# RMSNorm statistics of a decoder trunk: token rows in pieces of 128, 128 and 8 instead of three times 88

## Chip, cores and metric

The kernel runs on one core of one Trainium2 chip. The metric is the device time of one execution in microseconds, the median over several runs. A profiled execution gives, beside its time, a trace of every instruction of that core.

## What is computed

One inference step of a four-layer decoder trunk over 256 prompt tokens and 8 decode tokens, 264 in all, with a model width of 1024 and float32 weights. Each layer has three sublayers: a half feed-forward block, a token mixer (short convolution, sparse attention, differential attention, convolution again, by layer), and a second half feed-forward block. There are 12 sublayers. Each has an RMSNorm ahead of it and one behind it, which makes 24 norms:

```python
def rms_norm(x, g):
    xf = x.astype(jnp.float32)
    y = xf * lax.rsqrt(jnp.mean(xf * xf, axis=-1, keepdims=True) + EPS)
    return (y * g.astype(jnp.float32)).astype(x.dtype)

def half_ffn(x, g_pre, g_post, w_in, w_out):
    gate, up = jnp.split(rms_norm(x, g_pre) @ w_in, 2, axis=-1)
    return x + 0.5 * rms_norm((jax.nn.silu(gate) * up) @ w_out, g_post)
...
        xp = xp + rms_norm(yp, g[3])
        xs = xs + rms_norm(ys, g[3])
```

The norm's scale is one number per token, `rsqrt(mean of squares + EPS)`.

## The kernel before

**Layout.** Activations stand with the model width on the 128 partitions, in 8 chunks, and the 264 tokens along the free dimension. A sublayer is a row of matrix products with tokens as the moving operand. Weights stream in from memory in units of 512 columns by four chunks. ScalarE rounds each unit to a high part (`w_high_ring`), VectorE subtracts to get the low part (`w_low_ring`, line 864), and TensorE forms each product from three matmuls, high by high, high by low, low by high (lines 1391 to 1393). All engines follow programs written out by hand in five blocks, one per engine, that meet at semaphores. The order within an engine is the order of its program.

**A norm in five steps.** Each norm has a number: even ones are the norm ahead of a sublayer (the pre norm), odd ones the norm behind it (the post norm).

- *Statistics*, TensorE, `norm_stats`, line 1399. The squares summed over chunks (`sum_pre` or `sum_post`, plus for a post norm the last chunk of `sq`) are the stationary operand, and a column of 1/1024 (`mean_col`) is the moving one. The result is a column of token means in PSUM, tokens on partitions. The 264 tokens are cut into three columns of `NT` = 88 rows. A post norm does this twice, once for `sum_post` and once for `sq`. Each float32 matmul leaves two records in the profile, so three matmuls are six records.
- *Variance*, VectorE, `norm_var`, line 908. One instruction adds EPS to the 88 by 3 block and signals `var_ready`.
- *Power*, GpSimd (POOL in the profile), line 618. One instruction raises the 88 by 3 block to the power -1/2 into `rs` and signals `rs_ready`. GpSimd's program does the norms in order, and ahead of a pre norm's power it adds up the squares of `x` chunk by chunk (line 584).
- *Broadcast*, TensorE, `norm_bcast`, line 1408. For each third of the tokens, a matmul with the `rs` column repeated 128 times as the stationary operand and the identity as the moving one puts every token's scale on all 128 partitions, tokens along the free dimension again. Only the last of the three signals `bcast_done`.
- *Use*, VectorE. For a pre norm, `norm_copy` (lines 914 and 915) copies the scales from PSUM to `r_pre`, and the drains of the first products multiply with it. For a post norm, line 1365 scales `y` straight from PSUM, and line 1371 adds it to `x`.

**What stands around them.** A pre norm works beside products: the statistics follow the products of the sublayer's first group, and the broadcast stands in TensorE's program behind the first 48 matmuls of the second group. VectorE forms two more low parts (line 864) between the variance and the copy. A post norm is a dead end: nothing of the next sublayer can start before `x` is updated. TensorE runs matmuls that nobody reads (`keep_running`, line 1415), 9 ahead of the broadcast and 13 behind it.

Of the kernel before, what the change touches and what calls it, by code (L numbers as in the profile page):

```python
# [26 lines left out]
ALU = mybir.AluOpType  # L27
# [3 lines left out]
P = 128  # L31
D_MODEL = 1024
SEQ = 256
DEC = 8
T = SEQ + DEC
# [8 lines left out]
EPS = 1e-6  # L44
# [78 lines left out]
def trunk_kernel(nc, x_prompt, x_sample, state_conv, cache_nsa, state_nsa_win, cache_diff, page_table,  # L123
# [12 lines left out]
    with ctx:  # L136
# [333 lines left out]
        def bcast_out(norm, k):  # L470

            b = norm_bank(norm)
            if norm % 2:
                return ps[:, b, 8 + NT * k:8 + NT * k + NT]
            return ps[:, b + k // 2, 320 + NT * (k % 2):320 + NT * (k % 2) + NT]

        tok_stores = {"nsa": 6, "diff": 9}

# [34 lines left out]
        @block.gpsimd  # L513
        def _(pool):
            fill = lambda t, v: nc.gpsimd.memset(t, v).then_inc(pool_step, 1)
            fill(ident[:, :], 0.0)
            pool.wait_ge(pool_step, 1)
            nc.gpsimd.affine_select(out=ident[:, :], in_=ident[:, :], compare_op=ALU.not_equal, fill=1.0, base=0,
                                    pattern=[[-1, P]], channel_multiplier=1).then_inc(ident_ready, 1)
            fill(cmp_ok[:, :, :], 1.0)  # L520
            fill(head_of_row[:, :], 1.0)
            fill(block_of_row[:, :], 1.0)
            fill(tmp[:, 0, 0:256], 0.0)
            fill(tmp[:, 1, 0:256], 0.0)
            fill(tmp[:, 2, 0:32], 0.0)
            fill(mean_col[:, 0:1], 1.0 / D_MODEL)
            fill(mean_col[:, 1:2], 1.0 / P)
            fill(minus_half[:, :], -0.5)
            fill(var[:, :], 1.0)
            fill(small[:, :], 1.0)  # L530
            fill(even_tmp[:, :], 0.0)
            n = [13]
            pool.wait_ge(pool_step, n[0])

            def select(t, pattern, op, fill, base, mult):

                nc.gpsimd.affine_select(out=t, in_=t, compare_op=op, fill=fill, base=base,
                                        pattern=pattern, channel_multiplier=mult).then_inc(pool_step, 1)
                n[0] += 1
                pool.wait_ge(pool_step, n[0])  # L540

            def copy(dst, src):
                nc.gpsimd.tensor_copy(dst, src).then_inc(consts_ready, 1)

            pool.wait_ge(ident_ready, 1)
            copy(ident_b[:, :], ident[:, :])

            select(tmp[:, 0, 0:P], [[-1, P]], ALU.is_ge, NEG, 0, 1)
            copy(causal[:, :], tmp[:, 0, 0:P])

            select(cmp_ok[:, :, :], [[P, 2], [-CMP_BLOCK, N_CMP]], ALU.is_ge, 0.0, -(CMP_BLOCK - 1), 1)
            nc.gpsimd.tensor_scalar(cmp_bias[:, :, :], cmp_ok[:, :, :], -1.0, -NEG, ALU.add, ALU.mult)\
                .then_inc(consts_ready, 1)

            select(head_of_row[:, :], [[-N_CMP, 16]], ALU.is_ge, 0.0, 0, 1)
            select(head_of_row[:, :], [[N_CMP, 16]], ALU.is_ge, 0.0, N_CMP - 1, -1)

            select(block_of_row[:, :], [[-CMP_BLOCK, 4]], ALU.is_ge, 0.0, 0, 1)
            select(block_of_row[:, :], [[CMP_BLOCK, 4]], ALU.is_ge, 0.0, CMP_BLOCK - 1, -1)
            fill(block_strip[:, :], 0.0)  # L560
            n[0] += 1
            pool.wait_ge(pool_step, n[0])
            copy(block_strip[:, 28:32], block_of_row[:, :])

            select(even_tmp[:, :], [[-2, 64]], ALU.not_equal, 1.0, 0, 1)

            view = tmp[:, 1, 0:256].rearrange("p (j n) -> p j n", n=N_CMP)
            select(view, [[-4, 32], [0, N_CMP]], ALU.is_ge, NEG, 0, 1)
            select(view, [[4, 32], [0, N_CMP]], ALU.is_ge, NEG, 3, -1)
            copy(own_cmp[:, :, :], view)  # L570

            view = tmp[:, 2, 0:32].rearrange("p (g b) -> p g b", b=DEC)
            select(view, [[-4, GROUPS], [-16, DEC]], ALU.is_ge, NEG, 0, 1)
            select(view, [[4, GROUPS], [16, DEC]], ALU.is_ge, NEG, 3, -1)
            copy(own_new[:, :, :], view)
            for norm in range(2 * len(subs)):
                s = subs[norm // 2]
                if norm % 2 == 0:

                    for c in range(1, NC):  # L580
                        pool.wait_ge(x_squared, NC * s.i + c + 1)
                        if c > 1:
                            pool.wait_ge(pre_summed, (NC - 1) * s.i + c - 1)
                        nc.gpsimd.tensor_tensor(sum_pre[:, :], sum_pre[:, :] if c > 1 else sq[:, 0, :], sq[:, c, :],
                                                ALU.add).then_inc(pre_summed, 1)
                if s.kind == "nsa" and norm % 2:

                    for b in range(s.cache_units):
                        t = stage_of["c", s.cache0 + b]
                        pool.wait_ge(loaded[t % RING], 32 * (t // RING + 1))  # L590
                        if b == 0:
                            pool.wait_ge(dec_q, s.attend + 1)
                        if b >= 2:
                            pool.wait_ge(cache_turned, pieces_to(s.cache0 + b - 2))
                        if b < DEC:
                            page = wstage[:, t % RING, :, :].rearrange("p (t g) (h c) -> p t (g h) c", t=2, c=256)
                            keys = page[:, :, :, 128:192]
                        else:
                            keys = wstage[:, t % RING, 0:2, :].rearrange("p t (g c) -> p t g c", g=GROUPS)[:, :, :, 0:HEAD]
                        nc.gpsimd.tensor_copy(k_pairs[:, b % 2, :, :, :], keys).then_inc(keys_paired, 1)  # L600
                if s.cache_units and norm % 2:

                    pool.wait_ge(at_scaled, task0[s.kind] + len(TASKS[s.kind]))
                    pool.wait_ge(tok_stored, 16 * tok_stores[s.kind])
                    nc.gpsimd.memset(pt_wide[0][:, :, :], 0.0).then_inc(wide_zeroed, 1)
                    if s.kind == "nsa":
                        pool.wait_ge(cache_scored, pieces_to(2 * DEC - 1))
                        nc.gpsimd.memset(pt_wide[1][:, :, :], 0.0).then_inc(wide_zeroed, 1)
                if s.kind == "diff" and norm % 2:

                    pool.wait_ge(sub_var, 1)
                    nc.gpsimd.tensor_tensor(sub_r, sub_v, minus_half[:, 0:16], ALU.pow).then_inc(sub_rs, 1)
                    pool.wait_ge(sub_var, 2)
                    nc.gpsimd.tensor_tensor(s_nmx[0][0:64, :], s_mx[0][0:64, :], minus_half[0:64, 0:1], ALU.pow)\
                        .then_inc(sub_rs, 1)

                pool.wait_ge(var_ready, norm + 1)
                nc.gpsimd.tensor_tensor(rs[0:NT, :], var[0:NT, :], minus_half[0:NT, 0:3], ALU.pow).then_inc(rs_ready, 1)  # L618


        @block.scalar
# [237 lines left out]
        def _(dve):  # L859
# [44 lines left out]
            def norm_var(norm):  # L904

                dve.wait_ge(stats_done, norm + 1)
                b, col = norm_bank(norm), stat_col(norm)
                V.tensor_scalar(var[0:NT, :], ps[0:NT, b, col:col + 3], EPS, None, ALU.add).then_inc(var_ready, 1)  # L908

            def norm_copy(s):  # L910

                dve.wait_ge(bcast_done, 2 * s.i + 1)
                b = norm_bank(2 * s.i)
                V.tensor_copy(r_pre[:, 0:2 * NT], ps[:, b, 320:320 + 2 * NT]).then_inc(rstd_ready, 1)
                V.tensor_copy(r_pre[:, 2 * NT:T], bcast_out(2 * s.i, 2)).then_inc(rstd_ready, 1)
                dve.wait_ge(rstd_ready, 2 * (s.i + 1))

            def low_x(s, c):
# [463 lines left out]
        def _(pe):  # L1382
# [12 lines left out]
            def norm_stats(norm, squares, first=True, last=True):  # L1395

                b, col = norm_bank(norm), stat_col(norm)
                for k in range(3):
                    mm = MM(ps[0:NT, b, col + k:col + k + 1], squares[:, NT * k:NT * k + NT], mean_col[:, 0:1],
                            start=(norm % 2 == 1 and first and k == 0), stop=last, skip_group_check=True)  # L1400
                if last:
                    mm.then_inc(stats_done, 1)

            def norm_bcast(norm):

                pe.wait_ge(rs_ready, norm + 1)
                for k in range(3):
                    mm = MM(bcast_out(norm, k), rs[0:NT, k:k + 1].broadcast_to([NT, P]), ident[0:NT, 0:NT],  # L1408
                            start=(norm % 2 == 1 and k == 0), stop=True, skip_group_check=True)
                mm.then_inc(bcast_done, 1)  # L1410

# [596 lines left out]
```

## Time and profile before

| what | value |
|---|---|
| median of 3 runs | 2265.44 us (2263.7 to 2267.54) |
| the profiled execution's own time | 2265.54 us |
| its span, first to last instruction | 2263.8 us |
| TensorE matmuls busy | 2175.4 us (96% of the span) |
| VectorE busy | 1447.8 us (64%) |
| ScalarE busy | 948.4 us (42%) |
| GpSimd busy | 173.4 us (8%) |
| mean granted TensorE clock | 0.991 of full speed |

The busy time of an engine counts each moment once, however many instructions overlap in it. Matmuls overlap their neighbours, so the duration of one is more than the time that it adds to the stream. For the norms, the timeline of one norm says more than the busy shares: a step costs what lies between its start and the start of the step that waits for it.

### The profile page before, as it was taken

The page shows a single profiled execution, that of the slowest core. Times are in us where ns is not written, and L with a number is a line of the kernel's source. Part 1 is how long each engine was busy: PE and PEld are TensorE (multiplying, and loading weights), DVE is VectorE, ACT ScalarE, POOL GpSimd, SP SyncE. Part 2 cuts the span into 40 slices and gives each one's busy share as a digit, 9 for nine tenths or more (in the row PEclk, how much of TensorE's full clock was granted, in tenths as well). Part 3 has the DMA queues.
Part 4 walks back from the last instruction along what each step waited for, and adds up shares of the span by engine and source line. Part 5 has one row for each costly group of instructions (what it writes and reads, how often), then busy time and mean ns, then how long its engine had stood idle before and what let it go on. Part 6 is the DMA issues. An engine that isn't in the chain of part 4 may idle for free.

```text
span 2263.8 us, 42724 instructions
## 1 busy us (share of the span) xinstructions
PE 2175.4 (96%) x17890; PEld 2091.6 (92%) x17890; DVE 1447.8 (64%) x1677; ACT 948.4 (42%) x1111; POOL 173.4 (8%) x165
## 2 busy tenths in 40 slices
PE   7999999999999989999999999779999999999997
PEld 7999999999999955799999999469999999999997
DVE  6764877647755568477567646657765765677753
ACT  4434354434444335344445434325444444435432
POOL 3000120002001000020020002002001100202000
PEclk9999999999999999999999999999999999999999
DMA  7554446554653543455455554324654654455550
GB/s 229 188 189 147 164 151 211 173 179 151 200 176 123 177 132 122 160 162 195 153 165 189 176 182 163 131 73 133 197 184 140 202 183 163 142 186 169 185 179 27
DMA packets 286125, 370.83 MB, mean 164 GB/s; under 512 B 12247, under 2 KB 212360, under 8 KB 285924
## 3 DMA queue, kind: packets, MB, share of 16 engines
q1 hardware_dynamic: 282378, 364.57, 48.9%
q10 hardware_dynamic: 3610, 4.28, 0.5%
q8 instruction: 105, 1.72, 0.3%
q14 instruction: 32, 0.26, 0.0%
HBM read 364.87 MB, written 8.11 MB: 165 GB/s over the span
## 4 chain that ended last, share of the span: by engine, by line
PE 45%; issue 9%; DVE 8%; ACT 1%; POOL 1%; POOLq 0%; DVEq 0%; ACTq 0%
PE ps L1391 13%; PE ps L1393 13%; PE ps L1392 13%; DVE y L1365 1%; DVE x L1371 1%; PE ps L1613 1%; DVE probs L1141 1%; DVE kt_dec L1194 1%; DVE w_low_ring L864 1%; PE ps L1603 1%; PE ps L1570 1%; ACT w_high_ring L634 1%; PE ps L1408 0%; POOL rs L618 0%; DVE small L1127 0%
## 5 line engine op out<-in xcount | busy, mean ns | idle before, releaser
L864 DVE TENSOR_TENSOR w_low_ring<-wstage,w_high_ring 128x2048 fp32r<-128x2048 f32 x332 | 732.1, 2230 | 280.8 <-ACT w_high_ring L634 200.9
L1391 PE MATMUL ps<-x_hi,w_high_ring 128*128 128x264 f32 x3112 | 888.4, 285 | 3.5 <-DVE w_low_ring L864 3.5
L1393 PE MATMUL ps<-x_hi,w_low_ring 128*128 128x264 f32 x3112 | 884.9, 284 | 0.0
L1392 PE MATMUL ps<-x_lo,w_high_ring 128*128 128x264 f32 x3112 | 883.7, 284 | 0.0
L1391 PEld LDWEIGHTS ps<-x_hi,w_high_ring 128*128 128x128 f32 x3112 | 586.5, 188 | 4.1 <-issue 4.1
L1392 PEld LDWEIGHTS ps<-x_lo,w_high_ring 128*128 128x128 f32 x3112 | 588.0, 189 | 0.0
L1393 PEld LDWEIGHTS ps<-x_hi,w_low_ring 128*128 128x128 f32 x3112 | 586.8, 189 | 0.0
L1391 PE MATMUL ps<-h_hi,w_high_ring 128*128 128x264 f32 x1664 | 473.5, 285 | 0.6 <-issue 0.6
L1393 PE MATMUL ps<-h_hi,w_low_ring 128*128 128x264 f32 x1664 | 473.8, 285 | 0.0
L1392 PE MATMUL ps<-h_lo,w_high_ring 128*128 128x264 f32 x1664 | 472.4, 284 | 0.0
L634 ACT ACTIVATE w_high_ring<-wstage 128x2048 fp32r<-128x2048 f32 (+2 forms) x172 | 307.9, 1817 | 306.9 <-PE ps L1393 288.8
L1391 PEld LDWEIGHTS ps<-h_hi,w_high_ring 128*128 128x128 f32 x1664 | 313.1, 188 | 1.2 <-issue 1.2
L1392 PEld LDWEIGHTS ps<-h_lo,w_high_ring 128*128 128x128 f32 x1664 | 313.9, 189 | 0.2 <-issue 0.2
L1393 PEld LDWEIGHTS ps<-h_hi,w_low_ring 128*128 128x128 f32 x1664 | 313.3, 188 | 0.0
L805 ACT ACTIVATE w_high_ring<-wstage 128x2048 fp32r<-128x2048 f32 x160 | 302.1, 1907 | 16.3 <-PE ps L1393 16.1
L641 ACT ACTIVATE tmp<-tmp 128x528 f32<-128x528 f32 x88 | 57.0, 648 | 398.9 <-DVE tmp L888 398.9
L618 POOL TENSOR_TENSOR rs<-var,minus_half 88x3 f32<-88x3 f32 x24 | 68.5, 2853 | 1704.9 <-DVE var L908 1704.9
L643 ACT ACTIVATE h_hi<-tmp 128x528 f32 (+1 forms) x88 | 56.8, 646 | 144.6 <-DVE tmp L898 144.6
L888 DVE TENSOR_TENSOR tmp<-ps,r_pre 128x528 f32<-128x528 f32 x88 | 62.1, 706 | 82.3 <-PE ps L1393 82.1
L901 DVE TENSOR_TENSOR h_lo<-tmp,h_hi 128x528 f32 (+1 forms) x88 | 62.4, 709 | 81.5 <-ACT h_hi L643 81.5
L1444 PE MATMUL ps<-x_hi,w_high_ring 128*128 128x264 f32 x384 | 99.0, 288 | 7.0 <-ACT x_hi L649 3.8
L1445 PE MATMUL ps<-x_hi,w_low_ring 128*128 128x264 f32 x384 | 97.8, 285 | 0.0
(285 smaller groups left out, 1827.3 us busy)
## 6 DMA issues: line engine op xcount, KB each, us to landing
wstage<-in_ffn_w_in_dram SPq DMA_DIRECT2D x352, 512.0 KB, 5.1
wstage<-in_ffn_w_out_dram SPq DMA_DIRECT2D x160, 512.0 KB, 4.6
wstage<-in_conv_w_in_dram SPq DMA_DIRECT2D x48, 512.0 KB, 4.8
wstage<-in_nsa_w_in_dram SPq DMA_DIRECT2D x20, 512.0 KB, 4.9
wstage<-in_ffn_w_out_dram SPq DMA_DIRECT2D x32, 256.0 KB, 2.8
wstage<-in_conv_w_out_dram SPq DMA_DIRECT2D x16, 512.0 KB, 5.0
wstage<-in_cache_nsa_dram SPq DMA_DIRECT2D x16, 512.0 KB, 4.5
wstage<-in_diff_w_in_dram SPq DMA_DIRECT2D x16, 512.0 KB, 5.2
```

Of the source, the lines that this page charges most:

```text
L618: nc.gpsimd.tensor_tensor(rs[0:NT, :], var[0:NT, :], minus_half[0:NT, 0:3], ALU.pow).then_inc(rs_ready, 1)
L634: nc.scalar.activation(w_high_ring[:, u % RING, 0:n, 0:cols], wstage[:, t % RING, 0:n, 0:cols], ACT.Copy).then_inc(w_high, 1)
L641: nc.scalar.activation(tanh_t, gate_t, ACT.Tanh, scale=0.5).then_inc(tanh_done, 1)
L805: nc.scalar.activation(w_high_ring[:, u % RING, :, :], wstage[:, t % RING, :, :], ACT.Copy).then_inc(w_high, 1)
L864: V.tensor_tensor(w_low_ring[:, u % RING, 0:n, 0:cols], wstage[:, stage_of["w", u] % RING, 0:n, 0:cols], w_high_ring[:, u % RING, 0:n, 0:c ...
L888: V.tensor_tensor(gate_t, ps[:, 4 * psum_set:4 * psum_set + 2, 0:T], b3(r_pre[:, :], 2), ALU.mult)\
L901: V.tensor_tensor(h_lo[:, chunk, :], prod_t, h_hi[:, chunk, :].bitcast(F32), ALU.subtract)\
L1391: MM(out, wh, hi, start=first, stop=False)
L1392: MM(out, wh, lo, start=False, stop=False)
L1393: return MM(out, wl, hi, start=False, stop=last)
L1444: MM(out(tile), w(w_high_ring, tile), x_hi[:, c, :], start=(c == 0), stop=False)
L1445: MM(out(tile), w(w_low_ring, tile), x_hi[:, c, :], start=False, stop=False)
```

## The change

The tokens are cut as the rest of the kernel cuts them, by `TOK`: prompt tokens 0 to 127, prompt tokens 128 to 255, and the 8 decode tokens. Columns 0 and 1 of `var` and `rs` then have 128 rows, and column 2 has 8 rows. The variance is two VectorE instructions, the 8 by 1 block first, then 128 by 2. The power is two GpSimd instructions, 128 by 2 first, then 8 by 1, each with its own signal. The power still waits for both variance instructions. The first two broadcast matmuls wait for the first power, the last one for the second.

```diff
         def bcast_out(norm, k):
 
             b = norm_bank(norm)
+            t0, n = TOK[k]
             if norm % 2:
-                return ps[:, b, 8 + NT * k:8 + NT * k + NT]
-            return ps[:, b + k // 2, 320 + NT * (k % 2):320 + NT * (k % 2) + NT]
+                return ps[:, b, 8 + t0:8 + t0 + n]
+            return ps[:, b + (k > 0), 320 + P * (k > 1):320 + P * (k > 1) + n]
...
-                pool.wait_ge(var_ready, norm + 1)
-                nc.gpsimd.tensor_tensor(rs[0:NT, :], var[0:NT, :], minus_half[0:NT, 0:3], ALU.pow).then_inc(rs_ready, 1)
+                pool.wait_ge(var_ready, 2 * (norm + 1))
+                nc.gpsimd.tensor_tensor(rs[:, 0:2], var[:, 0:2], minus_half[:, 0:2], ALU.pow).then_inc(rs_ready, 1)
+                nc.gpsimd.tensor_tensor(rs[0:DEC, 2:3], var[0:DEC, 2:3], minus_half[0:DEC, 0:1], ALU.pow)\
+                    .then_inc(rs_ready, 1)
...
-                V.tensor_scalar(var[0:NT, :], ps[0:NT, b, col:col + 3], EPS, None, ALU.add).then_inc(var_ready, 1)
+                V.tensor_scalar(var[0:DEC, 2:3], ps[0:DEC, b, col + 2:col + 3], EPS, None, ALU.add).then_inc(var_ready, 1)
+                V.tensor_scalar(var[:, 0:2], ps[:, b, col:col + 2], EPS, None, ALU.add).then_inc(var_ready, 1)
...
-                V.tensor_copy(r_pre[:, 0:2 * NT], ps[:, b, 320:320 + 2 * NT]).then_inc(rstd_ready, 1)
-                V.tensor_copy(r_pre[:, 2 * NT:T], bcast_out(2 * s.i, 2)).then_inc(rstd_ready, 1)
+                V.tensor_copy(r_pre[:, 0:P], bcast_out(2 * s.i, 0)).then_inc(rstd_ready, 1)
+                V.tensor_copy(r_pre[:, P:T], ps[:, b + 1, 320:320 + T - P]).then_inc(rstd_ready, 1)
...
-                for k in range(3):
-                    mm = MM(ps[0:NT, b, col + k:col + k + 1], squares[:, NT * k:NT * k + NT], mean_col[:, 0:1],
+                for k, (t0, n) in enumerate(TOK):
+                    mm = MM(ps[0:n, b, col + k:col + k + 1], squares[:, t0:t0 + n], mean_col[:, 0:1],
                             start=(norm % 2 == 1 and first and k == 0), stop=last, skip_group_check=True)
...
-                pe.wait_ge(rs_ready, norm + 1)
-                for k in range(3):
-                    mm = MM(bcast_out(norm, k), rs[0:NT, k:k + 1].broadcast_to([NT, P]), ident[0:NT, 0:NT],
+                for k, (t0, n) in enumerate(TOK):
+                    pe.wait_ge(rs_ready, 2 * norm + (2 if n == DEC else 1))
+                    mm = MM(bcast_out(norm, k), rs[0:n, k:k + 1].broadcast_to([n, P]), ident[0:n, 0:n],
                             start=(norm % 2 == 1 and k == 0), stop=True, skip_group_check=True)
```

TensorE at a post norm, before, from the statistics to the first product of the next sublayer (a matmul's first operand here is the moving one, the second the stationary one, and the size is the output's):

```order
L1399 MATMUL ps<-mean_col,sum_post 88x1 [waits y_copied,post_added]
L1399 MATMUL ps<-mean_col,sum_post 88x1 x2
L1399 MATMUL ps<-mean_col,sq 88x1 [waits y_squared]
L1399 MATMUL ps<-mean_col,sq 88x1 x2
L1415 MATMUL ps<-own_cmp,ident_b 128x256 [waits y_copied]
L1415 MATMUL ps<-own_cmp,ident_b 128x256 x8
L1408 MATMUL ps<-ident,rs 128x88 [waits rs_ready]
L1408 MATMUL ps<-ident,rs 128x88 x2
L1415 MATMUL ps<-own_cmp,ident_b 128x256 x13
L1444 MATMUL ps<-x_hi,w_high_ring 128x264 [waits x_high,w_low,psum_drained]
```

The same place after the change:

```order
L1403 MATMUL ps<-mean_col,sum_post 128x1 [waits y_copied,post_added]
L1403 MATMUL ps<-mean_col,sum_post 128x1
L1403 MATMUL ps<-mean_col,sum_post 8x1
L1403 MATMUL ps<-mean_col,sq 128x1 [waits y_squared]
L1403 MATMUL ps<-mean_col,sq 128x1
L1403 MATMUL ps<-mean_col,sq 8x1
L1419 MATMUL ps<-own_cmp,ident_b 128x256 [waits y_copied]
L1419 MATMUL ps<-own_cmp,ident_b 128x256 x8
L1412 MATMUL ps<-ident,rs 128x128 [waits rs_ready] x2
L1412 MATMUL ps<-ident,rs 128x8 [waits rs_ready]
L1419 MATMUL ps<-own_cmp,ident_b 128x256 x13
L1448 MATMUL ps<-x_hi,w_high_ring 128x264 [waits x_high,w_low,psum_drained]
```

The number of matmuls stays, their shapes change, and the last broadcast matmul has a wait of its own. GpSimd, before, from the first pre norm on:

```order
L584 TENSOR_TENSOR sum_pre<-sq 128x264 [waits x_squared]
L584 TENSOR_TENSOR sum_pre<-sum_pre,sq 128x264 [waits pre_summed,x_squared] x6
L618 TENSOR_TENSOR rs<-var,minus_half 88x3 [waits var_ready] x2
L584 TENSOR_TENSOR sum_pre<-sq 128x264 [waits x_squared]
L584 TENSOR_TENSOR sum_pre<-sum_pre,sq 128x264 [waits pre_summed,x_squared] x6
```

And after the change:

```order
L585 TENSOR_TENSOR sum_pre<-sq 128x264 [waits x_squared]
L585 TENSOR_TENSOR sum_pre<-sum_pre,sq 128x264 [waits pre_summed,x_squared] x6
L619 TENSOR_TENSOR rs<-var,minus_half 128x2 [waits var_ready]
L620 TENSOR_TENSOR rs<-var,minus_half 8x1
L619 TENSOR_TENSOR rs<-var,minus_half 128x2 [waits var_ready]
L620 TENSOR_TENSOR rs<-var,minus_half 8x1
L585 TENSOR_TENSOR sum_pre<-sq 128x264 [waits x_squared]
```

A pair of instructions stands where one stood, and the second of the pair waits for nothing. On VectorE the pair of variance instructions (lines 911 and 912) stands where line 908 stood, with one wait ahead of the first.

## Rows read from the trace of the kernel before

**Rows 1.** The page: span, busy times, TensorE clock in 40 slices.
```profile
span 2263.8 us, 42724 instructions
PE 2175.4 (96%) x17890; PEld 2091.6 (92%) x17890; DVE 1447.8 (64%) x1677; ACT 948.4 (42%) x1111; POOL 173.4 (8%) x165
...
PEclk9999999999999999999999999999999999999999
```

**Rows 2.** Line 618, all 24 powers, and who waited for them.
```profile
L618 POOL TENSOR_TENSOR rs<-var,minus_half x24: 846/1850/5042, 35.8 to 2243.8; 88x3 f32<-88x3 f32 x24
...
  PEld ps L1408: 5.4, 12
  PE ps L1408: 2.1, 12
```

**Rows 3.** Waits: who waited for whom, us in total, times, longest.
```profile
DVE y L1365 <- PE ps L1408: 24.0, 12, 2.0
...
PE ps L1391 <- DVE w_low_ring L864: 3.5, 11, 0.3
```

**Rows 4.** Timeline, first post norm, TensorE matmuls: start us, us, instruction.
```profile
216.56 0.63 PE L1399 MATMUL ps<-mean_col,sum_post 128*88 128x1 f32 x6 [0.22 <-DVE sum_post L1356]
217.05 0.61 PE L1399 MATMUL ps<-mean_col,sq 128*88 128x1 f32 x6
217.52 1.14 PE L1415 MATMUL ps<-own_cmp,ident_b 128*128 128x256 bf16 x9
218.84 0.90 PE L1408 MATMUL ps<-ident,rs 88*128 88x88 f32 x6 [0.18 <-POOL rs L618]
219.58 1.58 PE L1415 MATMUL ps<-own_cmp,ident_b 128*128 128x256 bf16 x13
221.51 0.36 PE L1444 MATMUL ps<-x_hi,w_high_ring 128*128 128x264 f32 x1 [0.35 <-ACT x_hi L649]
```

**Rows 5.** Timeline, first post norm, TensorE weight loads.
```profile
216.56 0.54 PEld L1399 LDWEIGHTS ps<-mean_col,sum_post 128*88 128x88 f32 x6 [0.43 <-DVE sum_post L1356]
217.02 0.55 PEld L1399 LDWEIGHTS ps<-mean_col,sq 128*88 128x88 f32 x6
217.44 0.94 PEld L1415 LDWEIGHTS ps<-own_cmp,ident_b 128*128 128x128 bf16 x9
218.84 0.74 PEld L1408 LDWEIGHTS ps<-ident,rs 88*128 88x128 f32 x6 [0.46 <-POOL rs L618]
219.47 1.41 PEld L1415 LDWEIGHTS ps<-own_cmp,ident_b 128*128 128x128 bf16 x13
```

**Rows 6.** Timeline, first post norm, VectorE and GpSimd.
```profile
217.69 0.16 DVE L908 TENSOR_SCALAR var<-ps 88x3 f32<-88x3 f32 x1 [1.19 <-PE ps L1399]
219.86 0.49 DVE L1365 SCALAR_TENSOR_TENSOR y<-y,gains,ps 128x264 f32<-128x264 f32 x1 [2.01 <-PE ps L1408]
...
217.93 0.86 POOL L618 TENSOR_TENSOR rs<-var,minus_half 88x3 f32<-88x3 f32 x1 [179.31 <-DVE var L908]
```

**Rows 7.** Timeline, GpSimd, the two other powers of the program.
```profile
1502.40 2.93 POOL L612 TENSOR_TENSOR small<-small,minus_half 128x16 f32<-128x16 f32 x1 [8.97 <-DVE small L1295]
1512.91 0.54 POOL L614 TENSOR_TENSOR small<-small,minus_half 64x1 f32<-64x1 f32 x1 [7.58 <-DVE small L1308]
```

**Rows 8.** Timeline, GpSimd, instructions close behind one another.
```profile
2.24 0.12 POOL L515 MEMSET minus_half<- 128x32 f32 x1
2.30 0.10 POOL L515 MEMSET var<- 128x3 f32 x1
2.33 0.34 POOL L515 MEMSET small<- 128x288 f32 x1
...
18.16 2.08 POOL L584 TENSOR_TENSOR sum_pre<-sq 128x264 f32<-128x264 f32 x1 [9.46 <-ACT sq L650]
20.39 7.16 POOL L584 TENSOR_TENSOR sum_pre<-sum_pre,sq 128x264 f32<-128x264 f32 x6
```

**Rows 9.** Timeline, second pre norm, TensorE.
```profile
233.36 0.56 PE L1399 MATMUL ps<-mean_col,sum_pre 128*88 128x1 f32 x6
240.11 0.80 PE L1408 MATMUL ps<-ident,rs 88*128 88x88 f32 x6
```

**Rows 10.** Timeline, second pre norm, VectorE and GpSimd.
```profile
234.84 5.04 POOL L618 TENSOR_TENSOR rs<-var,minus_half 88x3 f32<-88x3 f32 x1 [3.82 <-DVE var L908]
...
234.61 0.16 DVE L908 TENSOR_SCALAR var<-ps 88x3 f32<-88x3 f32 x1
234.69 4.48 DVE L864 TENSOR_TENSOR w_low_ring<-wstage,w_high_ring 128x2048 fp32r<-128x2048 f32 x2
```

**Rows 11.** Third pre norm: GpSimd, then TensorE.
```profile
335.48 5.04 POOL L618 TENSOR_TENSOR rs<-var,minus_half 88x3 f32<-88x3 f32 x1 [3.20 <-DVE var L908]
...
341.37 0.80 PE L1408 MATMUL ps<-ident,rs 88*128 88x88 f32 x6
```

## The prediction

> **What bounds the kernel.** I read the page first, for the engines' shares. TensorE is busy 96% of the span at a clock in the top tenth throughout [rows 1], so most of the run is a stream of matmuls that the change doesn't touch. What the norms cost is what they add between two stretches of that stream. The view of line 618 says where: of the 24 powers only 12 have TensorE waiting for them [rows 2], and the waits show VectorE waiting 24.0 us in 12 pieces for the broadcast ahead of line 1365 [rows 3], 2.0 us for each of the 12 post norms. The timeline of one post norm shows the chain [rows 4, 6]: statistics from 216.56, variance at 217.69, power from 217.93 to 218.79, broadcast from 218.84, scaling at 219.86. That is 3.30 us, nearly all of it serial, and nothing useful runs beside it; TensorE fills its part with matmuls of line 1415 and then waits for `x_hi` until 221.51. So whatever the chain gains or loses is gained or lost twelve times, in full. The pre norms are read from two further timelines [rows 9 to 11].
>
> **The sum at a post norm**, term by term.
>
> *Statistics.* A matmul has two records. Their pace is set by the weight loads: twelve records with 88 weight columns take 217.44 - 216.56 = 0.88 us, 0.073 each, while six with 128 weight columns (the broadcast) take 219.47 - 218.84 = 0.63, 0.105 each [rows 5]. After the change there are eight records with 128 columns and four with 8: 8 x 0.105 = 0.84, plus four short ones, for which no row stands. Their bounds are 0 and 0.073 each. I take about the middle, 0.04, which makes 1.00 us and **+0.12 us**, with bounds of -0.04 and +0.25.
>
> *Variance.* Two VectorE instructions instead of one. At the second pre norm the next instruction starts 0.08 us behind the variance (234.61, then 234.69) though the variance lasts 0.16 [rows 10]. So the second one costs **+0.08**, at most 0.16.
>
> *First power.* The program has three sizes of power that run undisturbed: one element per partition in 0.54 us and sixteen in 2.93 [rows 7], three in 0.86 [rows 6], 0.846 at the least [rows 2]. The first two give 2.39 / 15 = 0.159 us per element, and from there 0.54 + 2 x 0.159 = 0.86 for three, as measured, though these rows have 64, 128 and 88 partitions. So partitions are free, and each power carries 0.38 us whatever its size. Two elements are 0.70 us: **-0.16**.
>
> *Second power.* 0.54 us by the nearest row, one element [rows 7]. Unlinked instructions on GpSimd start 0.06 us before their predecessor's record ends (2.24 + 0.12 against 2.30), and linked adds stand apart by 20.39 - (18.16 + 2.08) = 0.15 [rows 8]. The second power is unlinked: 0.54 - 0.05 = **+0.49**. The lower end is a single element's slope of 0.16 with the fixed part hidden; the upper end is a whole power of today's price behind a gap, 0.85 + 0.15 = 1.00.
>
> *Broadcast.* Today the scaling starts 219.86 - 218.79 = 1.07 us behind the power [rows 6]. After the change only the two records of the 8-token matmul stand behind the second power. Four records fewer are 4 x 0.105 = -0.42 [rows 5]. A moving operand of 8 columns also ends sooner: the statistics, with one moving column, release VectorE 0.17 us after TensorE has gone on to line 1415 (217.52 to 217.69), the broadcast with 88 columns 0.28 us (219.58 to 219.86) [rows 4, 6]. That is another -0.11, so **-0.53** in all, with bounds of -0.42 (nothing for the shorter operand) and -0.64 (one record's 0.105 more, should the two short records also follow closer).
>
> This term has a floor beneath it. The two prompt matmuls start 0.05 us behind the first power (218.79 to 218.84) and have four records, 4 x 0.105 + 0.02 = 0.44. The last matmul can't start earlier than 0.49 us behind the first power, so a second power shorter than 0.44 brings nothing more.
>
> The sum is 0.12 + 0.08 - 0.16 + 0.49 - 0.53 = **0.00 us** for each post norm. The low ends together, with the floor, are -0.04 + 0.08 - 0.16 + 0.44 - 0.64 = -0.32; the high ends 0.25 + 0.16 - 0.16 + 1.00 - 0.42 = +0.83. In words: the broadcast that is hidden was about as long as the fixed cost of the instruction that hides it.
>
> A rule of the Trainium skill speaks for more than this. The page "GPSIMD Engine Reference", section 2.1 (Instruction dispatch), says that completion doesn't hold back the next Pool instruction: each of the eight cores goes on as soon as its own share is done. By it the second power would begin inside the first one's record and cost well under its 0.49. No row here has two powers back to back, so the trace can't say. By the rule alone the sum would fall to the floor, 0.05 us lower per post norm and 0.6 us in all.
>
> **The pre norms.** The power lasts 5.04 us there instead of 0.85, and ends 0.71 us after VectorE's two low parts do (239.88 against 239.17) [rows 10]; VectorE, which then waits for the broadcast, takes up nothing between. So the power is held until these end, and the second power follows in a free stretch. The Trainium skill's page "SBUF — State Buffer", on engine ports, calls this an exclusive lock on a port pair that the two engines share; by that rule, the trace agrees. With the change, VectorE's low parts end 0.08 later, the first power is 0.16 shorter, and the second adds 0.49: `rs` is complete 0.41 us later, at 240.29. TensorE comes to the broadcast at 240.11 and to its last matmul four records later, 240.53 [rows 9]. The cover is 0.24 us. Two of the 12 pre norms are that tight; elsewhere, as at the third, the power ends 0.85 us ahead of TensorE [rows 11]. The longer statistics (six records, +0.06) fall into the 0.3 us that TensorE then waits for a low part, 11 times [rows 3]. The broadcast keeps six records at 128 weight columns. The two copies of 128 and 136 columns replace 176 and 88, the same sum. I cost the pre norms at **0**; if the cover went, 0.1 to 0.3 us each at a few of them.
>
> **Total.** 12 x 0.00 + 0 = 0. The sum is made against the profiled execution's 2265.54 us (span 2263.8), which is 0.1 us from the median of 2265.44. The forecast is **2265.5 us**.
>
> **The rivals.**
>
> *A. The second power costs a whole start.* GpSimd takes it up only when the first is done with, and its real price is near the upper end, 1.00 us. Everything else at my values, that is +0.51 per post norm, 12 x 0.51 = 6.1 us: 2271.6 us, slower. It decides from about 0.87 us for the second power, where 12 x 0.38 reaches 4.5 us. For it: the fixed part of 0.38 us is real. Against it: 0.54 us for one element already holds that part, and gaps on GpSimd are at most 0.15. Chance 9%.
>
> *B. The broadcast doesn't start behind the first power.* If the signal of the first power came only with the second, all six records would stand behind both, as today: the -0.53 falls away, +0.53 per post norm, 6.4 us: 2271.9 us. Nothing in the rows shows it; each instruction here releases its own waiter. Chance 4%.
>
> *C. The low ends meet.* Short statistics records, the floor reached, a short last broadcast: -0.32 per post norm, 3.8 us, 2261.7 us. For it: 8 weight columns may load in next to nothing. Against it: three terms would have to lie at their ends. To be beyond what can be measured it needs another 0.06 each. The chance that it goes that far, something that I don't see included, is 9%.
>
> **How the numbers follow.** A measurement of this kernel can tell about 0.2%, 4.5 us, from no change; that is 0.38 us per post norm, and my sum has to be wrong by that much, in one direction, at all twelve. The forecast of no measurable change has 78%, A and B together 13% (slower), C 9% (faster). The range takes in C nearly whole (-3.5 us) and reaches up to +4.8 us, since the unknown second power and the statistics can err further upward than down: 2262.0 to 2270.3 us. A's and B's own values lie outside and hold the rest.
>
> **What would show it.** In the changed profile a post norm should read: twelve statistics records in about 1.0 us; two variances 0.08 apart; a first power of 0.70; a second of 0.54 starting within 0.1 of the first one's end; four broadcast records beside it; line 1369 starting about 0.5 us behind the second power; and from the first statistics record to that line 3.3 us as before. The wait of VectorE for the broadcast should keep about 2.0 us. At pre norms TensorE should wait for no power. I'm wrong if the second power lasts clearly more than 0.54 or starts late, if the four prompt records begin only behind it, or if 12 pre norms show an idle TensorE ahead of line 1412.

## The result and the profile after

| what | before | after |
|---|---|---|
| median of 11 runs each | 2267.14 us | 2271.55 us |
| lowest and highest | 2263.33 to 2269.38 | 2269.47 to 2273.55 |
| profiled execution: time, span | 2265.54, 2263.8 us | 2273.55, 2271.8 us |
| mean granted TensorE clock | 0.991 | 0.990 |

The changed kernel is slower, by about a quarter of a percent: the ratio is 1.0027, with a 95% interval of 1.0018 to 1.0035. That is 6.1 us of 2267, between 4.1 and 7.9. (The recorded ratio isn't the quotient of the two medians. These lie 4.4 us apart, inside the same interval.) The profiled execution after is the slowest of its eleven, so its 8.0 us over the one before are partly scatter. Steps are compared below, not spans.

The first post norm after the change, TensorE's matmuls, then its weight loads (start us, us, instruction), which answer to [rows 4, 5]:

```profile
218.28 0.73 PE L1403 MATMUL ps<-mean_col,sum_post 128*128 128x1 f32 x6 [0.22 <-DVE sum_post L1360]
218.94 0.73 PE L1403 MATMUL ps<-mean_col,sq 128*128 128x1 f32 x6
219.60 1.16 PE L1419 MATMUL ps<-own_cmp,ident_b 128*128 128x256 bf16 x9
220.76 1.02 PE L1412 MATMUL ps<-ident,rs 128*128 128x128 f32 x6
221.71 1.59 PE L1419 MATMUL ps<-own_cmp,ident_b 128*128 128x256 bf16 x13
```

```profile
218.27 0.63 PEld L1403 LDWEIGHTS ps<-mean_col,sum_post 128*128 128x128 f32 x6 [0.43 <-DVE sum_post L1360]
218.93 0.63 PEld L1403 LDWEIGHTS ps<-mean_col,sq 128*128 128x128 f32 x6
219.59 0.88 PEld L1419 LDWEIGHTS ps<-own_cmp,ident_b 128*128 128x128 bf16 x9
220.75 0.93 PEld L1412 LDWEIGHTS ps<-ident,rs 128*128 128x128 f32 x6 [0.28 <-POOL rs L619]
221.71 0.33 PEld L1419 LDWEIGHTS ps<-own_cmp,ident_b 128*128 128x128 bf16 x4
```

The same place on VectorE and GpSimd, which answers to [rows 6]:

```profile
219.70 0.14 DVE L911 TENSOR_SCALAR var<-ps 8x1 f32<-8x1 f32 x1 [1.49 <-PE ps L1403]
219.78 0.14 DVE L912 TENSOR_SCALAR var<-ps 128x2 f32<-128x2 f32 x1
221.90 0.49 DVE L1369 SCALAR_TENSOR_TENSOR y<-y,gains,ps 128x264 f32<-128x264 f32 x1 [1.98 <-PE ps L1412]
...
219.99 0.71 POOL L619 TENSOR_TENSOR rs<-var,minus_half 128x2 f32<-128x2 f32 x1 [177.99 <-DVE var L912]
220.66 0.54 POOL L620 TENSOR_TENSOR rs<-var,minus_half 8x1 f32<-8x1 f32 x1
```

Variances, powers and signals did what was forecast: 0.08 us between the variances, a first power of 0.71 us, a second of 0.54 that starts 0.04 before the first one's end, and a broadcast that begins 0.06 behind the first power. Both surprises are on TensorE. The statistics take 219.70 - 218.28 = 1.42 us up to the variance, before 217.69 - 216.56 = 1.13. And the second power ends at 221.20, but the scaling starts only 0.70 us later, at 221.90, where 0.54 had been forecast.

The waits show the statistics over all 12 post norms (us in total, times, longest), after the change and then before it:

```profile
DVE y L1369 <- PE ps L1412: 23.6, 12, 2.0
DVE var L911 <- PE ps L1403: 19.2, 12, 1.8
```

```profile
DVE var L908 <- PE ps L1399: 16.4, 12, 1.7
```

VectorE waits 19.2 us ahead of the variance instead of 16.4, 2.8 more. Its wait for the broadcast shrinks from 24.0 to 23.6 [rows 3], but the second variance stands ahead of it: from first variance to scaling the median of twelve is 2.183 us against 2.155.

The third pre norm, after the change, and one further row of the kernel before, which follows its broadcast of [rows 11]:

```profile
343.79 0.92 PE L1412 MATMUL ps<-ident,rs 128*128 128x128 f32 x6
344.64 0.39 PE L1395 MATMUL ps<-x_hi,w_high_ring 128*128 128x264 f32 x1
344.87 0.28 PE L1396 MATMUL ps<-x_lo,w_high_ring 128*128 128x264 f32 x1
```

```profile
341.95 0.37 PE L1391 MATMUL ps<-x_hi,w_high_ring 128*128 128x264 f32 x1
```

The view shows no wait of TensorE here, and yet its broadcast takes 344.64 - 343.79 = 0.85 us of the product stream where it took 341.95 - 341.37 = 0.58. Counted to the second product behind the broadcast, the median of the 12 pre norms is 1.077 us against 0.794: +0.283.

So the loss has three places: the statistics of the post norms, 2.8 us in all; variance to scaling, 12 x 0.028 = 0.3; the broadcasts of the pre norms, 12 x 0.283 = 3.4. Together 6.5 us, against 6.1 by the ratio.

### The profile page after: what moved, and what is told of

Same layout as the page of the kernel before. It is cut to its first block, busy times and chain, and to the rows that moved or that the text cites. A ratio compares the mean times of both kernels' runs of the same rounds, so it can differ in the third digit from the quotient of the medians.

```text
span 2271.8 us, 42772 instructions
## 1 busy us (share of the span) xinstructions
PE 2187.5 (96%) x17890; PEld 2100.3 (92%) x17890; DVE 1449.8 (64%) x1701; ACT 948.8 (42%) x1111; POOL 183.9 (8%) x189
## 4 chain that ended last, share of the span: by engine, by line
PE 53%; DVE 8%; issue 1%; ACT 1%; POOL 0%; DVEq 0%; ACTq 0%
PE ps L1395 16%; PE ps L1397 16%; PE ps L1396 16%; DVE y L1369 1%; PE ps L1617 1%; DVE x L1375 1%; DVE kt_dec L1198 1%; DVE probs L1145 1%; DVE w_low_ring L867 1%; PE ps L1574 1%; PE ps L1607 1%; PE ps L1412 1%; PE ps L1419 1%; ACT w_high_ring L637 1%; PE ps L1403 0%
## 5 line engine op out<-in xcount | busy, mean ns | idle before, releaser
L619 POOL TENSOR_TENSOR rs<-var,minus_half 128x2 f32<-128x2 f32 x24 | 64.9, 2704 | 1706.8 <-DVE var L912 1706.8
```

Source lines behind the costliest of these rows:

```text
L619: nc.gpsimd.tensor_tensor(rs[:, 0:2], var[:, 0:2], minus_half[:, 0:2], ALU.pow).then_inc(rs_ready, 1)
```

## The experiments

Two theories went into the first four runs. *Theory S*, shape: a float32 matmul with 8 contraction rows costs TensorE 0.1 to 0.2 us where it follows one with 128 rows, and again where one with 128 follows it. *Theory W*, waits: the cost lies in the second power and the extra semaphore wait.

**The last broadcast with 128 contraction rows.** `rs` is filled with ones once at the start, the moving identity is 128 rows by 8 columns, and the result is the same.

```diff
+            fill(rs[:, :], 1.0)
...
-                    mm = MM(bcast_out(norm, k), rs[0:n, k:k + 1].broadcast_to([n, P]), ident[0:n, 0:n],
+                    mm = MM(bcast_out(norm, k), rs[:, k:k + 1].broadcast_to([P, P]), ident[:, 0:n],
```

> The changed kernel, but the last broadcast matmul contracts over all 128 rows of rs (rows beyond the 8 hold ones, and the identity's columns leave them out of the result). Theory S (a float32 matmul with 8 contraction rows between matmuls with 128 costs 0.1 to 0.2 us at each of the two changes): in pre norms the broadcast to the second record after it falls from 1.08 us to about 0.80, as before the change; in post norms the last matmul starts as soon as the second power is done (0.05 us behind it, now 0.20) and the scaling line starts 2.0 us behind the variance, not 2.18. In all 12 x (0.27 + 0.15) = 5 us less than the changed kernel, about 2266.5 us, level with the kernel before. Theory W (the extra wait and the second power are the cost): nothing moves, 2271.6 us.

Measured: median 2265.98 us, ratio to before 0.9999 (0.9990 to 1.0008). The third pre norm of this kernel:

```profile
343.00 0.73 PE L1413 MATMUL ps<-ident,rs 128*128 128x128 f32 x6
343.58 0.37 PE L1396 MATMUL ps<-x_hi,w_high_ring 128*128 128x264 f32 x1
343.79 0.28 PE L1397 MATMUL ps<-x_lo,w_high_ring 128*128 128x264 f32 x1
```

The same six records take 0.58 us of the stream again. To the second product it is 0.79 us, and variance to scaling falls to 2.058. A matmul that contracts sixteen times as many rows is the cheaper one. Theory S holds in size, and theory W falls: the two powers and both waits are still there. The statistics are still 1.43 us, so this kernel should be some 1.6 us slower than before by its steps (+2.8 - 1.2); the runs can't resolve that.

**One wait for all three broadcast matmuls.**

```diff
+                pe.wait_ge(rs_ready, 2 * norm + 2)
                 for k, (t0, n) in enumerate(TOK):
-                    pe.wait_ge(rs_ready, 2 * norm + (2 if n == DEC else 1))
```

> The changed kernel, but all three broadcast matmuls wait once, for the second power. Theory S: pre norms stay as slow as after the change, since nothing there waits; post norms lose the overlap of four records with the power, and since these and the row change take 0.64 us and the power only 0.55, the scaling comes 0.5 us later: 12 x 0.5 = 6 us more, 2277.5 us. Theory W: pre norms get their 0.27 us back (3 us), and post norms pay the 0.5 us: 2274.5 us.

Measured: 2281.64 us, ratio 1.0071 (1.0057 to 1.0085). Nine of the twelve pre norms keep 1.077 us to the second product, so the wait isn't their cost. Variance to scaling is 2.694 instead of 2.183, 0.51 more, as expected: this is what the early start of the prompt columns is worth once the power is split. But 12 x 0.51 = 6.1 us, and the median rose by 10.

Part of the rest is at the three other pre norms, the first, the second and the eleventh. The second reads (GpSimd, then TensorE):

```profile
243.18 0.54 POOL L620 TENSOR_TENSOR rs<-var,minus_half 8x1 f32<-8x1 f32 x1
...
243.42 0.28 PE L1397 MATMUL ps<-x_hi,w_low_ring 128*128 128x264 f32 x1
243.77 1.02 PE L1412 MATMUL ps<-ident,rs 128*128 128x128 f32 x6
```

Behind the product of line 1397 nothing starts for 0.35 us, where the next matmul otherwise starts 0.12 behind. The broadcast waits for the second power, which ends at 243.72, and then takes 0.10 us longer: 0.34 us in all. The eleventh loses the same and the first 0.64, together 1.3 us. So the trace accounts for 7.4 us.

> The kernel with one wait once more, with a profile. Its median was 10 us over the changed kernel's, while its trace gives 12 x 0.51 = 6.1 us. If the rest is time at half clock that some executions get and the first profiled one did not, this profile shows more half-clock time than the 49 us of the first. If it shows the same and the time is again near 2281, the rest stays open.

Measured again: 2281.54 us (two runs). The profile shows the same 49 us at half clock, and all norms as in the first one. So that explanation falls, and about 3 us stay open. They may be scatter: the intervals of the two ratios leave the 10 us uncertain by about 4, and in single executions the stage of sparse attention alone took from 224 to 229 us, from variance to variance, in the profiles without extra matmuls.

**The cut alone, one power.** The power is one instruction of 128 by 3 (`var` holds ones in the rows not used).

```diff
-                nc.gpsimd.tensor_tensor(rs[:, 0:2], var[:, 0:2], minus_half[:, 0:2], ALU.pow).then_inc(rs_ready, 1)
-                nc.gpsimd.tensor_tensor(rs[0:DEC, 2:3], var[0:DEC, 2:3], minus_half[0:DEC, 0:1], ALU.pow)\
-                    .then_inc(rs_ready, 1)
+                nc.gpsimd.tensor_tensor(rs[:, :], var[:, :], minus_half[:, 0:3], ALU.pow).then_inc(rs_ready, 1)
...
+                pe.wait_ge(rs_ready, norm + 1)
                 for k, (t0, n) in enumerate(TOK):
-                    pe.wait_ge(rs_ready, 2 * norm + (2 if n == DEC else 1))
```

> The cut in 128, 128 and 8 rows alone, with one power of 128 by 3 and one wait. Theory S: pre norms cost what they cost after the change (0.27 us more than before); in post norms the power is 0.85 instead of 0.70 and 0.54, and all six records stand behind it: variance to scaling 0.29 + 0.85 + 0.05 + 0.64 + 0.50 = 2.33 us against 2.18 after and 2.15 before: 12 x 0.15 = 1.8 us slower than the changed kernel, 2273.4 us. Theory W: with one power and one wait, as before the change: about 2268 us.

Measured: 2275.07 us, ratio 1.0038 (1.0024 to 1.0051). Variance to scaling is 2.336 us, 2.33 forecast; pre norms 1.077 as after the change. By its steps the cut alone costs more than the whole change, 12 x 0.153 = 1.8 us, so the split of the power is the good part of it. The times point the same way, but the intervals of the two ratios overlap. The power itself:

```profile
219.11 0.86 POOL L619 TENSOR_TENSOR rs<-var,minus_half 128x3 f32<-128x3 f32 x1 [179.86 <-DVE var L910]
```

Three elements on 128 partitions take 0.86 us, as on 88 [rows 6]: the 40 further partitions are free.

**The split alone, in thirds of 88.**

```diff
-                nc.gpsimd.tensor_tensor(rs[0:NT, :], var[0:NT, :], minus_half[0:NT, 0:3], ALU.pow).then_inc(rs_ready, 1)
+                nc.gpsimd.tensor_tensor(rs[0:NT, 0:2], var[0:NT, 0:2], minus_half[0:NT, 0:2], ALU.pow).then_inc(rs_ready, 1)
+                nc.gpsimd.tensor_tensor(rs[0:NT, 2:3], var[0:NT, 2:3], minus_half[0:NT, 0:1], ALU.pow).then_inc(rs_ready, 1)
...
-                pe.wait_ge(rs_ready, norm + 1)
                 for k in range(3):
+                    pe.wait_ge(rs_ready, 2 * norm + (2 if k == 2 else 1))
```

> The kernel before (three thirds of 88 rows) with the power in two instructions, 88 by 2 and 88 by 1, and the first two broadcast matmuls begun behind the first. Theory S: no small shapes, so pre norms as before; post norms: 0.24 + 0.70 + 0.51 + 0.05 + 0.11 to 0.18 + 0.39 = 2.00 to 2.07 us from variance to scaling against 2.155: 12 x 0.12 = 1.4 us less than before, 2265.7 us. Theory W: the split and the wait cost as in the change, 2270 us or more.

Measured: 2265.09 us, ratio 0.9992 (0.9983 to 1.0001). Its first post norm:

```profile
218.40 0.70 POOL L618 TENSOR_TENSOR rs<-var,minus_half 88x2 f32<-88x2 f32 x1 [177.51 <-DVE var L909]
219.06 0.55 POOL L619 TENSOR_TENSOR rs<-var,minus_half 88x1 f32<-88x1 f32 x1
...
218.16 0.16 DVE L909 TENSOR_SCALAR var<-ps 88x3 f32<-88x3 f32 x1 [1.19 <-PE ps L1400]
220.24 0.49 DVE L1366 SCALAR_TENSOR_TENSOR y<-y,gains,ps 128x264 f32<-128x264 f32 x1 [1.92 <-PE ps L1409]
```

220.24 - 218.16 = 2.08 us instead of 2.17: the idea of the change, without its shapes, gains a little in the trace. The median of the twelve is 2.077 against 2.155, a gain of 0.08 us where 0.12 had been expected.

> The kernel with 88-row thirds and the split power once more, since its first ratio, 0.9992, reached from 0.9983 to 1.0001. Its trace gives 2.078 us from variance to scaling against 2.155, so 12 x 0.077 = 0.9 us or 0.04%: a ratio near 0.9996, between 0.9987 and 1.0005. A ratio below 0.999 would say that the split gives more than the trace of one execution shows.

Measured again: 2264.76 us, ratio 0.9999 (0.9990 to 1.0008). The gain of 12 x 0.077 = 0.9 us is in the trace and can't be shown in the time. It is the fastest median of the study, and still no version that can be called faster than the kernel before.

**A table of shapes.** In the kernel before, ahead of each pre norm's broadcast, eight extra matmuls that nobody reads.

```diff
                 pe.wait_ge(rs_ready, norm + 1)
+                if norm % 2 == 0:
+                    k_rows, m_cols = ([(P, P), (8, P), (32, P), (64, P), (72, P), (88, P), (P, 8), (P, 32), (P, 64), (P, 88), (8, 8), (P, P)])[norm // 2]
+                    bank = norm_bank(norm) + 2
+                    for _ in range(4):
+                        MM(ps[0:m_cols, bank, 320:328], ident[0:k_rows, 0:m_cols], ident[0:k_rows, 0:8],
+                           start=False, stop=True, skip_group_check=True)
+                        MM(ps[:, bank, 336:344], ident[:, :], ident[:, 0:8], start=False, stop=True,
+                           skip_group_check=True)
```

> The kernel before, with eight extra matmuls (results unread) ahead of each pre norm's broadcast: four times a matmul of a given shape, each followed by one with 128 contraction rows and 128 stationary columns. The shape differs by norm: rows 128, 8, 32, 64, 72, 88 with 128 columns, then columns 8, 32, 64, 88 with 128 rows, then 8 by 8, then 128 by 128 again. Theory S: with 8 rows the start of the small one comes 0.20 us behind the last big record and the next big one 0.18 behind the small one, against 0.11; with 72 and 88 rows nothing. If what counts is the part of the array that is addressed, 32 and 64 rows cost as much as 8. The rival, that the cost grows as rows get fewer: 64 costs less than 32, and 32 less than 8, and 72 and 88 cost something.

This kernel ran once (2295.83 us), for its trace. Rows of its timeline, a pair of records each, for 8, 64 and 72 contraction rows, and for 64 stationary columns:

```profile
243.08 0.38 PE L1411 MATMUL ps<-ident 8*128 8x8 f32 x2
243.40 0.39 PE L1413 MATMUL ps<-ident 128*128 128x8 f32 x2
243.72 0.38 PE L1411 MATMUL ps<-ident 8*128 8x8 f32 x2
...
552.54 0.39 PE L1411 MATMUL ps<-ident 64*128 64x8 f32 x2
552.85 0.39 PE L1413 MATMUL ps<-ident 128*128 128x8 f32 x2
553.17 0.38 PE L1411 MATMUL ps<-ident 64*128 64x8 f32 x2
...
755.22 0.37 PE L1413 MATMUL ps<-ident 128*128 128x8 f32 x2
755.45 0.37 PE L1411 MATMUL ps<-ident 72*128 72x8 f32 x2
755.67 0.37 PE L1413 MATMUL ps<-ident 128*128 128x8 f32 x2
...
1586.85 0.28 PE L1411 MATMUL ps<-ident 128*64 128x8 f32 x2
1587.06 0.39 PE L1413 MATMUL ps<-ident 128*128 128x8 f32 x2
1587.38 0.28 PE L1411 MATMUL ps<-ident 128*64 128x8 f32 x2
```

With 8 rows a pair of matmuls takes 243.72 - 243.08 = 0.64 us, with 64 rows 0.63, with 72 rows 0.45. Between single records the trace shows 0.111 to 0.112 us at 72, 88 and 128 rows, and at 8, 32 and 64 rows alike 0.18 to 0.19 at each change of shape and 0.13 behind it. So of the sizes tried it doesn't count how few the rows are, only on which side of a border between 64 and 72 they lie. Small stationary operands cost a change too: with 64 columns a pair takes 0.53 us though its own load is shorter, with 8 columns 0.45 (a short load of 0.03 makes up for the change), with 88 columns 0.38. The rival, a cost that grows as rows get fewer, falls.

The Trainium skill, in "TensorEngine Tiling (Array Packing)", section Tiling Modes, lists modes of the array with tiles of 64 or 32 rows or columns, and says that changing the mode drains the engine. The border in the table agrees. That a matmul which asks for no tiling enters such a mode is inferred from this border, and that a drain is what the 0.2 us at a change consist of is argued, not shown: the runs show the shapes and the price.

**The 8-row matmul by itself, at all 12 pre norms**, with 8 rows and with 128 in the table's place. Nothing else differs.

> The same eight extra matmuls at all 12 pre norms, the small one with 8 rows. From the changed kernel's broadcast, 1.077 us against 0.791 with full rows, one such matmul costs 0.29 us. Theory S: 12 x 4 x 0.29 = 13.7 us more than the next kernel, at the same number of matmuls.

> The same eight extra matmuls, all with 128 rows: 16 records of about 0.08 to 0.11 us, 1.3 to 1.8 us per pre norm, all on TensorE's path: 15 to 21 us more than the kernel before, 2282 to 2288 us. Theory S has the kernel with 8 rows 13.7 us above this one; if rows were free, both would be equal.

Measured: 2308.95 us with 8 rows and 2289.14 with 128. The sign is theory S's, but the size is 19.8 us, not 13.7. (The kernel with 128 rows is 23 us above the kernel before, where 15 to 21 had been expected: its broadcast comes 1.71 us later and takes 0.08 longer, twelve times, 21.5 us.) The traces account for the difference in two parts. The eight matmuls take 0.84 us longer up to the broadcast, 12 x 0.84 = 10.0 us; so 0.21 per small matmul and not 0.29: with full rows the second record of such a matmul follows its first by 0.031 us in the full-row broadcast at pre norms, but by 0.112 in the probe, while with 8 rows it is 0.132 in both. Most of the rest is clock. Windows of 20 us about the second pre norm, with 8 rows and with 128 (us, busy by engine, then the granted clock):

```profile
240.00:260.00 20.00, 20.00 (x149) 19.72 (x148) 14.98 (x22) 5.74 (x4) 4.61 (x1) 0.91 0.59 193
```

```profile
240.00:260.00 20.00, 20.00 (x169) 20.00 (x168) 15.69 (x25) 5.76 (x3) 2.55 (x1) 1.00 0.55 182
```

Soon after its eight extra matmuls the first kernel ran part of the stream at the lower of the two levels, 1.2 GHz instead of 2.4, for 3.4 us. Over the run the clock records hold 67 us at that level against 53, and 14 us at half speed cost about 7. With the 10 that makes 17 of the 19.0 us by which the spans of the two profiled executions differ.

**No small shape at all.** The third column holds tokens 176 to 263, and the broadcast takes the last 8 of its 88 rows.

```diff
+                    if n == DEC:
+                        t0, n = T - NT, NT
...
+                    rows_n, cols = (NT, slice(NT - DEC, NT)) if n == DEC else (n, slice(0, n))
-                    mm = MM(bcast_out(norm, k), rs[0:n, k:k + 1].broadcast_to([n, P]), ident[0:n, 0:n],
+                    mm = MM(bcast_out(norm, k), rs[0:rows_n, k:k + 1].broadcast_to([rows_n, P]), ident[0:rows_n, cols],
```

The decode variance and power have 88 rows accordingly.

> The changed kernel, but its third column holds tokens 176 to 263 in 88 rows, of which only the last 8 are broadcast (identity columns 80 to 87). No shape is small any more, neither rows nor columns. Theory S: the broadcast as in the kernel with full rows (pre norms 0.79 us, variance to scaling 2.06). The statistics keep their 8 records with 128 stationary columns at 0.11 us and gain nothing: 1.41 us at a post norm, since a small column saves in its own load what it costs at the changes. So 2266 us. If the small columns were what made the statistics 0.29 us longer, they would fall to 1.14 and the time to 2263.

Measured: 2266.53 us, ratio 1.0003 (0.9994 to 1.0012). The broadcasts are as cheap as with 128 rows (0.791 us at pre norms, variance to scaling 2.072). The statistics of the feed-forward blocks are 1.40 us against 1.43, so they gain nothing from an even third piece. Against the kernel before they have eight records with 128 stationary columns, 0.112 us each, in the place of eight with 88 at 0.078: 8 x 0.034 = 0.27 us.

That doesn't clear the small columns. This kernel loads 128 + 128 + 88 stationary columns, the changed one only 128 + 128 + 8. Single records of the changed kernel's first post norm show where its saving went: the two records of the 8-column matmul stand 0.03 us apart, but the first starts 0.18 behind a 128-column record and the next 128-column record 0.09 behind the second. Over all twelve records the changes add about 0.28 us. Without them eight records at 0.112 and four at 0.03 would take 1.02 us, 0.08 more than twelve at 0.078. So in the statistics too the price is mostly that of the small shape, and the even piece pays the same price in longer loads.

## Why the prediction was wrong

I forecast 2265.5 us and no measurable change (78%), with a range up to 2270.3. The time lies above it. The terms at a post norm (medians of the twelve, the sum from unrounded terms):

| term | forecast | measured |
|---|---|---|
| statistics | +0.12 | +0.29 at the eight feed-forward blocks, +0.10 at the four mixers; mean 0.23 |
| variance | +0.08 | +0.05 |
| first power | -0.16 | -0.15 |
| second power | +0.49 | +0.51 |
| broadcast behind the power | -0.53 | -0.39 |
| sum | 0.00 | +0.26 |
| pre norms, each | 0 | +0.28 |

12 x 0.26 + 12 x 0.28 = 6.5 us.

- *The bound was read rightly.* What a post norm loses is lost in full, and the GpSimd terms came out within 0.02 us. The model of 0.38 us per power and 0.16 per element, free of partitions, held for every new size. The second power starts 0.03 to 0.04 us before the first one's record ends and keeps its 0.54 us. So the further overlap of two powers, for which the prediction had a rule beside its sum, did not come.
- *The step that failed* is one sentence at the pre norms: "The broadcast keeps six records at 128 weight columns", costed at 0. I priced a matmul by its stationary columns alone and never asked what its 8 contraction rows would do. The same blind spot sits in the broadcast term. The last matmul can start only 0.20 us behind the fourth prompt record (four records, then the change), which is later than the end of the second power. So the floor of 0.49 us behind the first power was really 0.70, TensorE and not the power set the end, and the term was 0.14 too good. Not all of that floor is the shape: with full rows the last matmul starts 0.60 us behind the first power, since the first two prompt records stand 0.21 apart. But there the term is -0.51, nearly the forecast, so the shape makes 0.12 of the 0.14.
- *A part of the price stood in the trace of before*, in rows that I hadn't taken: the transposes of the input, where the 8 decode tokens follow 128 prompt tokens.

```profile
11.09 0.49 PEld L1459 LDWEIGHTS ps<-ident,tok_in 8*128 8x128 f32 x3 [0.33 <-issue]
11.91 0.49 PEld L1459 LDWEIGHTS ps<-ident,tok_in 8*128 8x128 f32 x3 [0.33 <-issue]
```

Ahead of each load with 8 rows the loads stand idle for 0.33 us, put down to "issue", and in this stretch no load with more rows does. Not all of it is lost, since loads elsewhere run ahead of the matmuls. In the single matmul records an 8-row transpose starts 0.35 us behind the 128-row one, where a 128-row one starts 0.27 behind another. That is 0.09 us each, as in the broadcast (0.205 against 0.112).

- *The statistics* were mis-sized, mostly by the same step. That the pace is set by weight loads held: 0.105 us per record with 128 columns was 0.112, 0.073 with 88 was 0.078, and the short ones, taken at 0.04, stand 0.03 apart. But the changes to 8 columns and back, about 0.28 us over the twelve records, had no place in the sum. The measured 0.29 lies just above my bound of +0.25. The four mixers lose only 0.10; there the statistics of `sq` already waited for ScalarE before (0.7 us in four pieces), which covers part.
- *The rivals.* A and B forecast the right time, 2271.6 and 2271.9, by mechanisms that the trace refutes: the second power is 0.54 us, and the prompt records start 0.06 behind the first. C didn't occur. No rival had a cost on TensorE that comes from a shape.
- *The pre norms' cover* held: in the changed kernel's trace TensorE waits for no power at eleven of them and about 0.02 us at the first, and this was the only danger that I had named. The kernel with one wait shows how thin it was: there three pre norms do wait.

## What to carry to other kernels

Cutting work along its natural edges (128, 128, 8) can cost more than even pieces (88, 88, 88) when a piece has 64 rows or columns or fewer: here a float32 matmul of 8 rows between full ones cost 0.28 us, with sixteen times as many rows 0, and in the table the price ended between 64 and 72 rows. If a short piece can't be avoided, contract over full rows with the surplus masked by the moving operand. And before a matmul's shape is priced, look for the same shape in the trace of before, and compare the starts of single records there. Idle time called "issue" ahead of one shape alone is a hint, not yet the price.

## What the runs showed that I had not expected

The first pre norm after the change has a second power of 2.07 us instead of 0.54:

```profile
37.26 2.70 POOL L619 TENSOR_TENSOR rs<-var,minus_half 128x2 f32<-128x2 f32 x1 [9.75 <-DVE var L912]
39.93 2.07 POOL L620 TENSOR_TENSOR rs<-var,minus_half 8x1 f32<-8x1 f32 x1
...
37.11 4.47 DVE L867 TENSOR_TENSOR w_low_ring<-wstage,w_high_ring 128x2048 fp32r<-128x2048 f32 x2
```

VectorE's two low parts run to 41.58. Here the first power got in between them and ended at 39.96, and the second ended only at 42.00, so by these times it was held by the other one. The single power of the kernel before had got in between at the same place (2.84 us, in the timeline of its first pre norm). In the eleven others the first power waited for both low parts, and the second ran free. So splitting an instruction on GpSimd can make it wait twice beside VectorE. It cost next to nothing here, since the change of shape takes as long: the broadcast's records span 0.68 us at this norm and 0.67 at the others. In the kernel with full rows the same norm takes 1.00 us to the second product instead of 0.79.

And matmuls of changing shape may cost twice. In the kernel with 8-row matmuls a stretch of 3.4 us at half clock begins within 2 us of the extra matmuls' end at seven of the twelve pre norms, in its twin with full rows at one. Over the whole run the difference is smaller, 67 us against 53, and each figure is from one execution. The table's kernel has such a stretch behind 72 rows and none behind 64, so that the changes of shape bring it on is not shown.
